# Routed feed-forward of a two-layer decoder trunk: four vector adds, one narrow product and three scatter products change places

## What is computed

```python
def moe_swiglu(h, w_router, b_router, w_gate_up, w_down):
    probs = jax.nn.softmax(logits, axis=-1)
    top_p, top_i = lax.top_k(probs, 2)
    top_p = top_p / jnp.sum(top_p, axis=-1, keepdims=True)
    gates = ...                       # (tokens, 8), two entries a row
    for e in range(8):
        out = out + gates[:, e:e+1] * swiglu(tok, w_gate_up[e], w_down[e])

def swiglu(h, w_gate_up, w_down):     # inner width 3584
    gate, up = jnp.split(h @ w_gate_up, 2, axis=-1)
    return (jax.nn.silu(gate) * up) @ w_down
```

## Time and profile before

| | |
|---|---|
| median of 3 | 1531.9 us (1530.35 to 1533.28) |
| profiled execution | 1534.63 us, span 1532.9 us |
| granted clock of PE, mean | 0.949 |
| PE busy | 1383.5 us, 90% |
| DVE busy | 661.3 us, 43% |
| ACT busy | 498.7 us, 33% |
| DMA moved | 474.28 MB, mean 309 GB/s |

### The profile page before, as it was taken

The page is one execution under the profiler, slowest core; times in us unless marked ns, Lnnn a source line. Parts: engine busy times, 40 slices in busy tenths (PEclk is TensorE's granted clock), DMA queues, the critical chain, the costliest instruction groups (busy, mean ns, idle before and its releaser), DMA issues.

```text
span 1532.9 us, 25160 instructions
## 1 busy us (share of the span) xinstructions
PE 1383.5 (90%) x11083; PEld 976.7 (64%) x11084; DVE 661.3 (43%) x755; ACT 498.7 (33%) x557; POOL 34.8 (2%) x66
## 2 busy tenths in 40 slices
PE   3999999999999789899999899999797888988687
PEld 2763788888686545677777577767575565544343
DVE  5943444454400634765544555544665353200003
ACT  2323433434300512444443354433454352000001
POOL 2001000000100002000000000000000000000000
PEclk8989999999999998999999999999998899999889
DMA  8784884554664114559999969999989999999994
GB/s 296 298 316 176 314 346 165 196 188 169 244 246 165 55 51 170 204 216 410 411 411 413 406 234 410 412 410 414 410 340 412 411 412 413 410 411 413 412 413 171
DMA packets 206792, 474.28 MB, mean 309 GB/s; under 512 B 9986, under 2 KB 10030, under 8 KB 206670
## 3 DMA queue, kind: packets, MB, share of 16 engines
q1 hardware_dynamic: 199968, 470.83, 79.0%
q10 hardware_dynamic: 6702, 1.71, 0.5%
HBM read 471.47 MB, written 1.05 MB: 308 GB/s over the span
## 4 chain that ended last, share of the span: by engine, by line
PE 66%; DMA 14%; SPq 11%; DVE 4%; ACT 2%; issue 1%; ACTq 1%; POOL 0%; DVEq 0%
PE ps L2269 34%; SPq L488 11%; DMA ring<-in_moe_w_down_dram 10%; PE ps L2550 7%; PE ps L2562 5%; PE ps L2352 4%; DMA ring<-in_moe_w_gate_up_dram 2%; DMA ring<-in_ada_w_dram 2%; PE ps L2416 2%; PE ps L2245 2%; PE ps L2360 2%; PE ps L2080 2%; DVE ring_lo L1836 1%; DVE arena L1235 1%; PE ps L2144 1%
## 5 line engine op out<-in xcount | busy, mean ns | idle before, releaser
L1836 DVE TENSOR_TENSOR ring_lo<-ring,w 128x2048 fp32r<-128x2048 f32 x126 | 288.4, 2289 | 196.1 <-ACT w L1005 154.1
L1005 ACT ACTIVATE w<-ring 128x2048 fp32r<-128x2048 f32 x126 | 240.6, 1913 | 233.4 <-PE ps L2269 209.3
L2550 PE MATMUL ps<-ring,arena 128*32 128x128 f32 (+1 forms) x5376 | 253.2, 299 | 40.6 <-DMA ring<-in_moe_w_gate_up_dram 32.8
L2550 PEld LDWEIGHTS ps<-ring,arena 128*32 128x32 f32 (+1 forms) x5376 | 189.8, 117 | 104.7 <-issue 45.0
L2269 PE MATMUL ps<-ring_lo,x_hi 128*128 128x512 f32 x560 | 219.4, 392 | 0.0
L2269 PE MATMUL ps<-w,x_hi 128*128 128x512 f32 x336 | 136.4, 406 | 7.1 <-DVE arena L1783 5.5
L1475 DVE TENSOR_TENSOR ring_lo<-ring,w_hi 128x2048 fp32r<-128x2048 f32 x42 | 95.6, 2290 | 85.9 <-ACT w_hi L765 85.9
L2269 PE MATMUL ps<-w,x_lo 128*128 128x512 f32 x336 | 132.1, 393 | 0.0
L2269 PEld LDWEIGHTS ps<-ring_lo,x_hi 128*128 128x128 f32 x560 | 105.9, 189 | 20.3
L2562 PE MATMUL ps<-ring,tri 128*32 128x512 f32 (+1 forms) x448 | 75.7, 693 | 28.0 <-DMA ring<-in_moe_w_down_dram 26.5
L765 ACT ACTIVATE w_hi<-ring 128x2048 fp32r<-128x2048 f32 x42 | 78.8, 1909 | 50.3 <-PE ps L2269 42.1
(11 more groups left out here) (391 smaller groups left out, 1560.6 us busy)
## 6 DMA issues: line engine op xcount, KB each, us to landing
ring<-in_moe_w_gate_up_dram SPq DMA_DIRECT2D x112, 2048.0 KB, 17.2
ring<-in_moe_w_down_dram SPq DMA_DIRECT2D x56, 2048.0 KB, 18.2
ring<-in_ada_w_dram SPq DMA_DIRECT2D x24, 2048.0 KB, 10.8
ring<-in_ffn_w_gate_up_dram SPq DMA_DIRECT2D x14, 2048.0 KB, 12.2
ring<-in_ffn_w_down_dram SPq DMA_DIRECT2D x7, 2048.0 KB, 7.9
ring<-in_sb_w_qkv_dram SPq DMA_DIRECT2D x6, 2048.0 KB, 8.6
ring<-in_s_w_out_dram SPq DMA_DIRECT2D x2, 2048.0 KB, 7.7
ring<-in_sb_w_out_dram SPq DMA_DIRECT2D x2, 2048.0 KB, 13.7
```

The source lines that it names most:

```text
L1005: act.activation(half3(h).bitcast(F32R), ff_half(gran(pair_place(*main_granule(n))), half), ACT.Copy).then_inc(whi_done, 1)
L1836: dve.tensor_tensor(ff_half(ring_lo[place % RING][:, :], half).bitcast(F32R), ff_half(gran(place), half), half3(h), ALU.subtract).then_inc ...
L2550: ins = pe.matmul(dst[width * r:width * r + width, 0:cols], x[:, k, 0:width], weights[:, k, cols * r:cols * r + cols], start=k == 0, stop= ...
```

## The change

In wide and light bodies the four `add_scattered` of a pair's rows move on DVE from the next pair's body into the end of the pair that scatters them, behind `x_rest`. Pair 0 keeps them where they were, for the rows that are zero at the start. `keep_pair_weights` moves ahead of `w_rest(3)`. On PE `tail_down(0)` moves behind `main_up(0)` and `gather_second`. In `pair_end`, `scatter_first` moves ahead of `second_turn` and the product of bd6. No instruction is added or removed.

```diff
@@ pair_end, DVE
                 if p + 1 < PAIRS:
                     x_rest(p + 1, 1)
+                    for i in range(4):
+                        add_scattered(p + 1 + PAIRS, i)
@@ pair_wide, DVE
                     w_rest(2 * n + 2)
                     if f == 0:
-                        for i in range(4):
-                            add_scattered(p + PAIRS, i)
+                        if p == 0:
+                            for i in range(4):
+                                add_scattered(PAIRS, i)
+                        keep_pair_weights(p)
                     w_rest(2 * n + 3)
-                    if f == 0:
-                        keep_pair_weights(p)
                     w_rest(2 * n + 4)
                     product_main(f)
@@ pair_end, PE
+                scatter_first(p)
                 second_turn(p, FB - 1, width)
                 second_down(p, FB - 1, width)
-                scatter_first(p)
                 scatter_pair(p)
@@ pair_wide, PE
                         pair_weights(p)
-                    tail_down(f)
+                    if f:
+                        tail_down(f)
                     main_up(f)
                     if f == 0:
                         gather_second(p)
+                        tail_down(f)
```

## The result

| | before | after |
|---|---|---|
| median | 1533.56 us (7 runs) | 1539.06 us (7 runs, 1537.46 to 1541.59) |
| ratio to before, 95% | | 1.003 (1.0017 to 1.0042) |
| span of the profiled execution | 1532.9 us | 1536.3 us |

The changed kernel is slower by 0.3%, some 4.6 us, and by 5.5 us in the medians. Its median of 1539.06 us lies 0.3 us inside the upper end of the forecast's range; 1.7 us of its distance from the 1536.8 put is that before's own median was 1531.9 in three runs and 1533.56 in seven. The page of the kernel after, cut to its span and two lines of its 40 slices, has the same picture as before: a stream of weights at 409 GB/s and more in every slice of the experts' part but for its start, the starts of pairs and the end.

A forecast was written before the change was run, and what follows sets the result against it. The weight stream bounds the experts' part, empty only where a pair begins. Terms 3.25 - 2.95 - 0.95 + 0.8 = +0.15 us plus 4.8 of clock give +4.95: median 1536.8 us, forecast's own range 1534.1 to 1539.4, with (a) and (c) 1530.6 to 1539.5.

The forecast's parts named there:

- The bound and what carries over: Experts' part: weight stream bounds; shifts up to main_up(1)'s end move everything later, gains behind it go to DMA waits.
- d1: Shift of main_up(1) in pair 1: wait of 6.17 us hidden, half returning as new idle; -2.95 us.
- Rival (c): Pair 0: the stream absorbs its delay, so d0 drops out; -0.7 us, 1531.2 us; chance 0.10.
- The trap in the move: Tail bodies, ahead of main_turn(0): late tail_down(0) holds w_rest(4) and product_main(0) on DVE; PE idle for 3.1 us.
- rival (b): Behind tail_down(0): no idle, as w_rest(4) doesn't really hold product_main(0); -6.85 us, 1525.1 us; chance 0.07.
- d0: Shift of main_up(1) in pair 0: later turn plus 0.4 us behind it; +3.25 us with the clock held.
- d2: Shift in pair 2: main_gate(0) later but covered by ad0's wait, main_down(0) earlier; -0.95 us, clock held.
- e: Kernel's end: PE waits for the copy of bd6's results ahead of scatter_pair; +0.8 us.
- The clock: Four new idles in pairs 0, 1 and 2 lower PE's clock: 2 x 1.3 + 2 x 1.1 = +4.8 us.
- Rival (a): The clock holds in all four new idles; +0.15 us, 1532.1 us; chance 0.20.
- Case (d): All four idles cost their upper ends and pair 2's cover is gone; +11.2 us, 1543.1 us; chance 0.07.
- The sum: Whole kernel: +0.15 us with the clock held plus 4.8 us of clock, +4.95 us.

The follow-up runs named there:

- mid: Changed kernel with tail_down(0) between main_up(0) and gather_second instead of behind both; ratio to before 0.9966 (0.9946 to 0.9986).
- mid_scat_old: Changed kernel with tail_down(0) between main_up(0) and gather_second, and scatter_first back behind bd6's product; ratio to before 0.9969 (0.9951 to 0.9986).
- scat_old: Changed kernel with scatter_first back behind bd6's product, all else as changed; ratio to before 1.0007 (0.9986 to 1.0027).
- only_tail: Kernel before with only tail_down(0) moved behind main_up(0) and gather_second; ratio to before 1.0097 (1.0074 to 1.012).
- only_adds: Kernel before with only the adds moved to the pair's end and the copy ahead of w_rest(3); ratio to before 1.0011 (0.9997 to 1.0025).
- mid_pad: mid_scat_old plus 14 idle transposes ahead of main_down(0) in the body without a tail; ratio to before 0.9958 (0.9943 to 0.9973).
- mid_pad_adds: mid_pad with the copy and w_rest(3) ahead of pair 0's adds on DVE; ratio to before 0.9944, 1525.3 us against 1535.0 beside it.
- tail_old: Changed kernel with tail_down(0) put back ahead of main_up(0), the rest as changed; ratio to before 1.0 (0.9978 to 1.0022).
- only_scat: Kernel before with only scatter_first moved ahead of second_turn; ratio to before 1.001 (0.9996 to 1.0025).
- warm: Changed kernel plus idle transposes in column 0: 22 ahead of main_turn(0) with a tail, 14 ahead of main_down(0) without; ratio to before 1.0025.
- after_again: Changed kernel profiled once more, unaltered; a single execution, 1536.53 us.

## Why the prediction was right, and where a term was wrong

**The bound and what carries over.** Right. What moved the end of a pair's `main_up(1)` moved everything behind it, in before, after and mid alike. Only that losses behind that point are taken back by waits for DMA doesn't hold in every case (see d1). mid took 3.3 and 5.9 us from stages 0 and 1 and its time fell by 0.64% against the change. Rival (c) is out.

**The trap in the move.** Right: DVE's `w_rest(4)` waited for L2565, `product_main(0)` behind it, and PE was idle for 3.08 us where 3.1 were put, in every execution that kept that order. mid removed it by moving one call, which also takes rival (b) away: the order on DVE held.

**d0.** Put at +3.25 us with the clock held, measured +3.29. The first idle was 2.79 us against 2.8.

**d1.** This is the step that failed. It was put at -2.95 us, -1.85 with its share of the clock, and stage 1 changed by -0.23 us. The hidden wait of 6.17 us is really hidden. The miss of 1.6 us is how late PE comes to pair 1. From pair 0's load to the end of `main_gate(0)` (SP's next x4 row) it was 861.88 - 675.15 = 186.73 us before and 866.67 - 677.37 = 189.30 after, so 2.6 us where I had 0.8. That is the whole miss: from the x4 row to the load behind it stage 1 gained 2.8 us, where the terms made 2.65 with the clock's 1.1 us in them. The other kernels split it. Six more without the scatter products' move (mid_scat_old, scat_old, only_tail, only_adds, mid_pad, mid_pad_adds) stand at 186.75 to 187.09; five with it (mid, tail_old, only_scat, warm, after_again) at 187.95 to 188.08. So that move costs pair 1 about 1.1 us (0.9 to 1.4), not 0.8: beside the copy, `tail_in` waits 0.8 instead of 0.5 us for ACT. The other 1.3 us is this one execution's, since after_again stands at 187.98. PE in pair 0, first in after, then in after_again:

```profile
798.42 2.40 PE L2565 MATMUL ps<-ring,tri 128*32 128x512 f32 x16 [2.17 <-DMA ring<-in_moe_w_down_dram]
```

```profile
795.86 1.92 PE L2565 MATMUL ps<-ring,tri 128*32 128x512 f32 x16 [1.31 <-DMA ring<-in_moe_w_down_dram]
```

In after the clock fell there: this product and the 24 matmuls behind it take 1.6 us more than in after_again (the wait itself ended 0.3 us earlier, so 1.3 are left), and the mean granted clock of the 10 us around them is 0.83 instead of 1.00. Five other executions, after_again among them, have a wait for a granule at this place, of 1.2 to 1.6 us and with the product behind it at full speed; after's is the longest and alone has slow work behind it. So a fall of the clock some 120 us behind the pair's start was passed on to pair 1. The prediction had the clock act only in the four new idles, and took PE's place against the stream at a pair's end as fixed. That after_again's stage 1 is 232.08 all the same is chance: it saves these 1.3 us and loses 1.5 to the clock in pair 1.

**d2.** Put at -0.95 and 1.3 us for the clock, in all +0.35. Measured -1.06 and +1.56, in all +0.50. Adds ahead of `w_rest(0)` delayed `main_gate(0)`, and ad0's landing covered it, but more narrowly than put. The slow matmuls behind the uncounted idle of 3.43 us brought `main_up(0)` 1.6 us later than the prediction had it, more than its 1.3 us to spare; PE reached the turn with no wait, and only DVE's `w_rest(5)` still decided. In mid, where `main_gate(0)` took 8.40 us, the chain that ended last runs over it and no longer over ad0.

**e.** Put at +0.8 us, measured +0.92 in stage 3; the kernels without the move stand at 398.5 to 399.6 us there, those with it at 400.3 to 401.4.

**The clock.** Put at +4.8 us over four idles. In the profiled execution it was 1.4 us in pair 1 and 1.6 in pair 2, and nothing in pair 0, so 3.0. In after_again pair 0 lost 4.1 us, pair 1 some 2.9 and pair 2 1.6, so about 8.6. The price had the right sign and lies between the two, but it is a spread, not a number. Rival (a), the clock holds in all four, is out: it fell in at least two of them in both profiles. Case (d) had been given 0.07, and after_again comes near it: its clock cost is as large as the 8.4 us of the four upper ends, and its stages sum to +9.9 us against 11.2; only pair 2's cover held. The upper end of 1.7 us for an idle ahead of the turn was too low: in after_again the one in pair 0 cost 2.5 us and the one in pair 1 some 2.9, because `main_down(0)` behind the narrow product began at the lower clock too.

**The sum.** In the profiled execution +4.5 us over the stages, against +4.95. Two terms that missed cancel in it: pair 0's clock was put 2.4 us too high, d1 1.6 us too low. That the total came within 0.5 us is luck; the second profile of the same kernel, by the same stages, stands at +9.9. The direction is not luck: it rests on the idle of 3.08 us, which was found where it was put, and on the kernels that removed it.

The Trainium skill's worked case in "TensorE: Matmul & The Clock Gate", section "HAM oscillation — how this bites in real kernels", gives about 26.7 us lost over 32 restarts, an estimate of 0.83 us for one. The restarts here cost more: pair 1 and pair 2 lost 1.4 and 1.6 us in the trace of after, and pair 0 in after_again 4.1 us over two.

## What to carry to other kernels

Before a product is moved out of a wait, list who waits for its semaphore and what is queued behind them: here one narrow product fed a step on DVE, behind which stood the step that PE needed next, and a place one call earlier (beside a gather of 3.5 us) turned a loss of 0.3% into a gain of 0.3%. Where a full stream of loads sets the pace, find the release that ends each hole in it and compare kernels from one such release to the next; that resolves single terms of 1 us which total times with a spread of 10 us can't. Take more than one profile of a kernel before a stage is called better or worse: the clock alone moved single stages of the changed kernel by 1 to 4 us here. Work that hides nothing when it is done early, as the first scatter products here, may have been hiding a copy where it stood.

## What the runs showed of the hardware that I had not expected

- The same idle may or may not cost TensorE's clock. Ahead of `main_up(0)` in pair 0 seven executions have an idle of 2.77 to 2.86 us. The 24 matmuls behind it take 5.7 to 5.8 us in five of them (after, mid, scat_old, mid_scat_old, warm) and 7.3 to 7.4 us in two (after_again, mid_pad), and after and after_again are the same kernel. With idle work in the gap ahead of the turn (warm), or without that gap (mid), no slow work stood behind it in pair 1.
- Behind 3.43 us of idle ahead of pair 2's `main_gate(0)`, nine of ten executions ran its 24 matmuls in 7.2 to 8.4 us, and one (mid_pad) in 5.7.
- In pair 2 the idle ahead of `main_down(0)` was 1.4 to 1.5 us in before, mid, only_tail and only_scat, and the way from there to pair 2's load was 19.4 to 19.5 us in all four. It was 2.15 us in after, after_again, tail_old, scat_old, only_adds and mid_scat_old, and the way was 20.9 to 22.3 us in all six. So kernels with 0.75 us more of idle there took 1.4 to 2.9 us longer; three of the six (scat_old, only_adds, mid_scat_old) also had 0.8 to 1.0 us of idle ahead of the turn, so the one idle is not the only difference.
